# A skewed expert loop in a mixture-of-experts layer: gate/up of the next expert, then down of this one

## The reference, cut to what is computed

```python
def moe(xn, router_w, router_b, w_gate_up, b_gate_up, w_down, b_down):   # xn: 512 rows of 1024
    ...   # top 4 of 32 experts per row, softmax over the four, rows sorted by expert
    def expert_block(args):
        xb, e = args
        h = xb @ w_gate_up[e] + b_gate_up[e]            # 1024 -> 2048, gate and up interleaved
        gate = jnp.minimum(h[:, ::2], SWIGLU_LIMIT)
        up = jnp.clip(h[:, 1::2], -SWIGLU_LIMIT, SWIGLU_LIMIT)
        act = (up + 1.0) * (gate * jax.nn.sigmoid(SWIGLU_ALPHA * gate))
        return act @ w_down[e] + b_down[e]              # 1024 -> 1024
    ...   # each row's four outputs, weighted, are added to it

def reference(x, ...):
    h = x + hybrid_mixer(rmsnorm(x, ...), ...)
    h = h + moe(rmsnorm(h, ...), ...)
    return rmsnorm(h, norm_final_g)
```

## Time and profile before

| what | before |
|---|---|
| median of 3 runs | 2169.55 us (2169.14 to 2170.2) |
| span of the profiled execution | 2170.8 us |
| PE busy | 1977.2 us, 91% of the span, 9156 matmuls |
| PEld, DVE, ACT busy | 74%, 68%, 55% of the span |
| DMA | 489.15 MB, mean 225 GB/s |
| expert stage on PE | first bias matmul at 869.88 us, last matmul at 2136.58 us |

### The profile page before, as it was taken

The page is one execution under the profiler, slowest core; times in us unless marked ns, Lnnn a source line. Parts: engine busy times, 40 slices in busy tenths (PEclk is TensorE's granted clock), DMA queues, the critical chain, the costliest instruction groups (busy, mean ns, idle before and its releaser), DMA issues. The chain is left out here.

```text
span 2170.8 us, 27072 instructions
## 1 busy us (share of the span) xinstructions
PE 1977.2 (91%) x9156; PEld 1610.2 (74%) x9157; DVE 1482.3 (68%) x1727; ACT 1183.8 (55%) x1102; POOL 107.7 (5%) x90
## 2 busy tenths in 40 slices
PE   4997899999999984999999999999999999999993
PEld 3885588888788874777777777777777777777772
DVE  3324344324532433899899898998998998989984
ACT  3333222223443221776777777777777777677772
POOL 0000000000000000000000100000001000000001
PEclk7999899989999995999999999999999999999997
DMA  4221122201023319899999999999999999999962
GB/s 159 78 77 40 60 77 97 92 0 54 1 78 97 136 47 343 294 333 334 322 339 330 328 333 331 332 330 330 339 329 324 344 329 329 333 327 336 337 232 83
DMA packets 148314, 489.15 MB, mean 225 GB/s; under 512 B 15392, under 2 KB 17056, under 8 KB 148080
## 3 DMA queue, kind: packets, MB, share of 16 engines
q1 hardware_dynamic: 139056, 471.79, 62.5%
q0 software_dynamic: 9216, 16.81, 3.1%
HBM read 482.24 MB, written 23.07 MB: 233 GB/s over the span
## 5 line engine op out<-in xcount | busy, mean ns | idle before, releaser
L1371 DVE TENSOR_TENSOR expert_lo<-expert_chunk,expert_hi 128x2048 fp32r<-128x2048 f32 x384 | 874.9, 2289 | 107.9 <-ACT expert_hi L1366 107.9
L1366 ACT CAST expert_hi<-expert_chunk 128x2048 fp32r<-128x2048 f32 x384 | 730.1, 1905 | 244.0 <-PE psum L1488 240.8
L1488 PE MATMUL psum<-expert_hi,rowsT_hi 128*128 128x512 f32 x1024 | 323.3, 397 | 2.0 <-DVE expert_lo L1371 2.0
L1488 PE MATMUL psum<-expert_lo,rowsT_hi 128*128 128x512 f32 x1024 | 317.5, 391 | 0.0
L1488 PE MATMUL psum<-expert_hi,rowsT_lo 128*128 128x512 f32 x1024 | 316.0, 390 | 0.0
L327 DVE TENSOR_TENSOR chunk_lo<-chunk,chunk_hi 128x2048 fp32r<-128x2048 f32 x48 | 109.9, 2290 | 277.9 <-ACT chunk_hi L323 277.9
L1488 PEld LDWEIGHTS psum<-expert_lo,rowsT_hi 128*128 128x128 f32 x1024 | 192.8, 188 | 41.9
L1488 PEld LDWEIGHTS psum<-expert_hi,rowsT_lo 128*128 128x128 f32 x1024 | 192.7, 188 | 41.7
L1488 PEld LDWEIGHTS psum<-expert_hi,rowsT_hi 128*128 128x128 f32 x1024 | 188.0, 189 | 38.4 <-DVE expert_lo L1371 2.7
L353 PE MATMUL psum<-chunk_hi,xT_hi 128*128 128x512 f32 x480 | 188.9, 394 | 1.6 <-PEq L131 1.6
L353 PE MATMUL psum<-chunk_hi,xT_lo 128*128 128x512 f32 x480 | 188.1, 392 | 0.0
(11 more groups left out here) (226 smaller groups left out, 2365.7 us busy)
## 6 DMA issues: line engine op xcount, KB each, us to landing
expert_chunk<-in_expert_w_gate_up SPq DMA_DIRECT2D x256, 1024.0 KB, 7.3
expert_chunk<-in_expert_w_down SPq DMA_DIRECT2D x128, 1024.0 KB, 6.9
chunk<-in_w_in SPq DMA_DIRECT2D x38, 1024.0 KB, 5.1
chunk<-in_w_branch_gla SPq DMA_DIRECT2D x4, 1024.0 KB, 5.1
chunk<-in_w_mix_out SPq DMA_DIRECT2D x4, 1024.0 KB, 5.1
x_sb<-in_x SPq DMA_DIRECT2D x4, 512.0 KB, 6.0
chunk<-in_w_branch_att SPq DMA_DIRECT2D x2, 1024.0 KB, 5.1
h_sb<-in_x SPq DMA_DIRECT2D x1, 2048.0 KB, 9.9
```

Source lines behind the costliest of these rows:

```text
L1366: act.copy(whi[j % self.SLOTS][:], raw[j][:]).then_inc(S["hi"], 1)
L1371: dve.tensor_tensor(wlo[s][:], raw[j][:], whi[s][:].bitcast(F32), ALU.subtract).then_inc(S["lo"], 1)
L1488: last = pe.matmul(bank, x[:, row, :], w[s][:, kk, i * COLS:(i + 1) * COLS], start=False, stop=(k == self.PER_HALF - 1 and kk == 1 and x i ...
```

## The change

Each turn of the loop (a body) does the eight gate/up chunks of expert e + 1 and then the four down chunks of expert e. Gate/up of expert 0 stands ahead of the loop, down of expert 31 behind it; 31 bodies lie between, two written out, 27 as nine turns of three, two written out. Around this:

- A gate/up chunk is one k-tile of 128 rows by all 2048 columns, read in pieces of 8 KB. It needs four PSUM banks at once (0 to 3). A down chunk is as before. Bytes, chunks and matmuls per expert are the same.
- The ring has 9 buffers in place of 12, there are 4 slots in place of 3.
- PE waits for the high part, does eight matmuls, then waits for the low part and does four.
- `swiglu_in`, `swiglu_p`, `swiglu_out` and `gate_sigmoid` work on 1024 columns at once, four instructions on DVE for sixteen, one on ACT for four. PE turns all eight blocks of activations after chunk q = 2 of the next body (`turn_act`).
- Rows are listed and gathered two experts ahead in place of one; so there are three index, weight and pick tiles. `rows_out`, which writes an expert's output for the scatter, comes after chunk q = 3 of the next body on ACT.

```diff
-                self.first_expert = [self.sem(f"expert_chunk_loaded{j}") for j in range(self.CHUNKS)]
-                self.expert_ring = [self.sb(moe, f"expert_chunk{j}", [P, 2, self.WIDE]) for j in range(self.CHUNKS)]
+                self.chunk_loaded = [self.sem(f"expert_chunk_loaded{j}") for j in range(self.RING)]
+                self.expert_ring = [self.sb(moe, f"expert_chunk{j}", [P, 2, self.WIDE]) for j in range(self.RING)]
...
-                for j in range(2):
-                    sp.dma_start(self.expert_ring[j][:], self.expert_weights(0, j)).then_inc(self.first_expert[j], 16)
+                for k in range(2):
+                    self.load_gate_up(sp, k, 0, k)
                 sp.wait_ge(S["hn_done"], NB)
                 sp.dma_start(self.normed.rearrange("(b p) n -> p b n", p=P), hn[:]).then_inc(S["stored"], 16)
-                for j in range(2, self.EARLY):
-                    sp.dma_start(self.expert_ring[j][:], self.expert_weights(0, j)).then_inc(self.first_expert[j], 16)
+                for k in range(2, self.GU):
+                    self.load_gate_up(sp, k, 0, k)
+                self.load_gate_up(sp, self.GU, 1, 0)
                 sp.wait_ge(S["stored"], 32)
...
-    CHUNKS, PER_HALF, SLOTS, WIDE = 12, 4, 3, 1024
-    EARLY = 9
+    CHUNKS, PER_HALF, WIDE = 12, 4, 1024
+    RING, SLOTS = 9, 4
+    GU, PER_BODY, UNROLL = 8, 12, 3
...
+    def body_chunk(self, e, q):
+        return self.GU + self.PER_BODY * e + q
+
+    def load_gate_up(self, sp, c, e, k):
+        src = self.t["expert_w_gate_up"][0][bass.ds(e, 1), k * P:(k + 1) * P, :]
+        self.load_chunk(sp, c, src.rearrange("a p (k n) -> p (a k) n", k=2))
+
+    def load_down(self, sp, c, e, q):
+        src = self.t["expert_w_down"][0][bass.ds(e, 1), 2 * q * P:(2 * q + 2) * P, :]
+        self.load_chunk(sp, c, src.rearrange("a (k p) n -> p (a k) n", p=P))
+
+    def load_chunk(self, sp, c, src):
+        r = c % self.RING
+        sp.dma_start(self.expert_ring[r][:], src).then_inc(self.chunk_loaded[r], 16)
...
+        def hi(act, c, i=0):
+            act.wait_ge(loaded[c % RING], 16 * (TURN // RING) * i + 16 * (c // RING + 1))
+            act.wait_ge(S["slots_free"], TURN * i + c + 1)
+            act.copy(whi[c % SLOTS][:], raw[c % RING][:]).then_inc(S["hi"], 1)
+
+        def lo(dve, c, i=0):
+            s = c % SLOTS
+            dve.wait_ge(S["hi"], TURN * i + c + 1)
+            dve.tensor_tensor(wlo[s][:], raw[c % RING][:], whi[s][:].bitcast(F32), ALU.subtract).then_inc(S["lo"], 1)
...
+        def gate_up_chunk(pe, c, i, k, u):
+            s = c % SLOTS
+            if k == 0:
+                for m, bank in enumerate(h_banks):
+                    pe.matmul(bank, pick[u][:], bias[:, m * COLS:(m + 1) * COLS], start=True, stop=False)
+            pe.wait_ge(S["hi"], TURN * i + c + 1)
+            for x in (x_hi, x_lo):
+                for m, bank in enumerate(h_banks):
+                    pe.matmul(bank, x[:, k, :], whi[s][:, m // 2, m % 2 * COLS:(m % 2 + 1) * COLS], start=False, stop=False)
+            pe.wait_ge(S["lo"], TURN * i + c + 1)
+            for m, bank in enumerate(h_banks):
+                last = pe.matmul(bank, x_hi[:, k, :], wlo[s][:, m // 2, m % 2 * COLS:(m % 2 + 1) * COLS], start=False,
+                                 stop=(k == KT - 1))
...
+        def body_pe(pe, e0, i):
+            e, more = i * self.UNROLL + e0, e0 < E - 2
+            for q in range(BODY):
+                c = self.body_chunk(e0, q)
+                if q == 0:
+                    pe.wait_ge(S["x_lo"], 2 * e + 4)
+                    pe.wait_ge(S["picked"], e + 2)
+                    pe.wait_ge(S["gu"], 2 * e + 2)
+                if q < GU:
+                    gate_up_chunk(pe, c, i, q, (e0 + 1) % 3)
+                else:
+                    if q == GU:
+                        pe.wait_ge(S["aT_lo"], 2 * e + 2)
+                        if more:
+                            pe.wait_ge(S["index"], 2 * e + 6)
+                        if e0:
+                            pe.wait_ge(S["y_out"], 2 * e)
+                    down_chunk(pe, c, i, q - GU, e0 % 3)
+                if q == 2:
+                    turn_act(pe, e)
+                if q == 3 and more:
+                    list_rows(pe, e + 2, late=e0 > 0)
+                if q == 9 and more:
+                    turn_rows(pe, e + 2)
...
+        def rows_out(act, e0, i, u):
+            e = i * self.UNROLL + e0
+            for m in range(2):
+                act.wait_ge(S["slots_free"], TURN * i + self.body_chunk(e0, BODY - 1) + 1 + SLOTS)
+                if e0:
+                    act.wait_ge(S["scattered"], 16 * e)
+                act.activation(y[:, m * COLS:(m + 1) * COLS], y_banks[m], ACT.Copy,
+                               scale=weight[u][:, 0:1]).then_inc(S["y_out"], 1)
+
+        def body_act(act, e0, i):
+            e = i * self.UNROLL + e0
+            for q in range(BODY):
+                hi(act, self.body_chunk(e0, q), i)
+                if q == 0:
+                    turned_hi(act, e + 1, S["x_turned"], S["x_hi"], x_hi)
+                if q == 1:
+                    gate_sigmoid(act, e, first=e0 == 0)
+                if q == 3 and e0:
+                    rows_out(act, e0 - 1, i, (e0 - 1) % 3)
+                if q == 7:
+                    turned_hi(act, e, S["act_turned"], S["aT_hi"], a_hi)
+
+
+
+        def swiglu_in(dve, e, c, i, first=False):
+            dve.wait_ge(S["slots_free"], TURN * i + c + 1 + SLOTS)
+            if not first:
+                dve.wait_ge(S["act"], e)
+            halves = lambda v: v[:].rearrange("p (b n) -> p b n", b=4)
+            dve.tensor_scalar(halves(gv), gates_ups[:, :, :, 0], SWIGLU_LIMIT, None, ALU.min).then_inc(S["gu"], 1)
+            dve.tensor_scalar(halves(uv), gates_ups[:, :, :, 1], SWIGLU_LIMIT, -SWIGLU_LIMIT, ALU.min,
+                              ALU.max).then_inc(S["gu"], 1)
+
+        def swiglu_p(dve, e):
+            dve.wait_ge(S["gu"], 2 * e + 2)
+            dve.scalar_tensor_tensor(out=uv[:], in0=uv[:], scalar=1.0, in1=gv[:], op0=ALU.add,
+                                     op1=ALU.mult).then_inc(S["p"], 1)
...
+        def body_dve(dve, e0, i):
+            e, more = i * self.UNROLL + e0, e0 < E - 2
+            for q in range(BODY):
+                lo(dve, self.body_chunk(e0, q), i)
+                if q == 0:
+                    turned_lo(dve, e + 1, S["x_hi"], S["x_lo"], x_hi, x_lo)
+                    swiglu_p(dve, e)
+                if q == 1:
+                    swiglu_out(dve, e, first=e0 == 0)
+                if q == 2 and more:
+                    list_hot(dve, e + 2)
+                if q == 7:
+                    turned_lo(dve, e, S["aT_hi"], S["aT_lo"], a_hi, a_lo)
+                    if more:
+                        list_index(dve, e + 2, (e0 + 2) % 3, reused=e0 > 0)
+                        pick_bias(dve, e + 2, (e0 + 2) % 3)
+                if q == 10:
+                    swiglu_in(dve, e + 1, self.body_chunk(e0, GU - 1), i)
...
+        PEELED, LAST = 2, E - 1
+        TURNS = (LAST - PEELED) // self.UNROLL
+
+        def over_bodies(engine, body):
+            for e0 in range(PEELED):
+                body(engine, e0, 0)
+            with engine.Fori(0, TURNS) as i:
+                for u in range(self.UNROLL):
+                    body(engine, PEELED + u, i)
+            for e0 in range(PEELED + self.UNROLL * TURNS, LAST):
+                body(engine, e0, 0)
...
+                def body(sp, e0, i):
+                    e = i * self.UNROLL + e0
+                    for q in range(BODY):
+                        c = self.body_chunk(e0, q)
+                        if c < RING:
+                            continue
+                        sp.wait_ge(S["lo"], TURN * i + c - RING + 1)
+                        if q < GU:
+                            self.load_gate_up(sp, c, e + 1, q)
+                        else:
+                            self.load_down(sp, c, e, q - GU)
+                over_bodies(sp, body)
+                for q in range(4):
+                    c = self.body_chunk(LAST, q)
+                    sp.wait_ge(S["lo"], c - RING + 1)
+                    self.load_down(sp, c, LAST, q)
...
+                first = self.body_chunk(LAST, 0)
+                hi(act, first)
+                gate_sigmoid(act, LAST)
+                rows_out(act, LAST - 1, 0, (LAST - 1) % 3)
+                for c in range(first + 1, first + 4):
+                    hi(act, c)
+                turned_hi(act, LAST, S["act_turned"], S["aT_hi"], a_hi)
...
+                pe.wait_ge(S["x_lo"], 2)
+                pe.wait_ge(S["picked"], 1)
+                for c in range(GU):
+                    gate_up_chunk(pe, c, 0, c, 0)
+                turn_rows(pe, 1)
+                over_bodies(pe, body_pe)
+                first = self.body_chunk(LAST, 0)
+                turn_act(pe, LAST)
+                pe.wait_ge(S["aT_lo"], 2 * E)
```

(3 more changed lines are left out.)

324 lines of the change are left out of this document (121 added, 203 removed).

## The result

| what | before | after |
|---|---|---|
| median | 2169.88 us (2169.14 to 2170.46, 4 runs) | 2266.19 us (2259.73 to 2269.28, 4 runs) |
| ratio, 95% interval | | 1.0439 [1.0422, 1.0456] |
| span of the profiled execution | 2170.8 us | 2257.6 us |
| POOL busy | 107.7 us | 512.6 us |

The changed kernel is 4.4% slower. The forecast, 2103 us with a range of 2095 to 2148, was wrong, and on the wrong side.

The account below looks back on a forecast made before the run. PE's own work plus its waits for the swiglu was taken as the bound. Start, 31 bodies of 36.9 us (1144) and end summed to 2070.1 against 2137.0, a gain of 66.9 us: forecast 2103 us, range 2095 to 2148.

Parts of the forecast that it names:

- Do the waits go?: Loop body: checked whether PE's waits all vanish, so that a body takes 36.9 us in place of 39.54.
- indices are ready at 18.6: Gather in the body: issued about 1 us later, landed at 27.6, wanted at 30.4; room 2.8 us, the tightest wait.
- four slots leave 8.2: Splits in the body: four slots give 8.2 us for a chunk's split, where three gave 5.45.
- 34.8 against 36.9: DVE's work per body, 34.8 us, against PE's 36.9; it fits with 2.1 us of room.
- small steps: PE's work per body: 0.14 us added to 36.77 for steps not resolved, giving 36.9.
- the order over four banks: PE's matmuls: between nothing and 1.0 us per body, 31 us in all; taken as nothing.
- Start: Ahead of the loop: PE begins at about 870.6 us, not 869.88; 5.7 us before the first body, turning covers 0.8.
- End: Behind the loop, ahead of the last down: 10.5 us with PE idle for all but 0.8.
- Rival 1: Loop transfers: DMA becomes the bound, a body takes 38.35 us, 2148 us in all; chance 0.20.
- rival 4: Gate/up loads: 8 KB pieces cost more engine time, a body 43.9 us, 2320 us in all; chance 0.06.
- Rival 2: Turning of rows: gather landing grows to 12 us, PE waits 1.2 a body, 2140 us in all; chance 0.07.
- Rival 3: DVE in the loop doesn't keep up, a body takes 39.5 us, 2170 to 2185 us in all; chance 0.04.

Follow-up runs that it names:

- the single fill: The changed kernel with one fill of a 128x1 tile on DVE behind the split of q = 3; 2102.2 us, ratio 0.9682 to the kernel before.
- the halves: The changed kernel with the single fill, and each chunk's load cut into two of half the size; 2102.66 us, ratio 0.9689 to the kernel before.
- three slots: The changed kernel with three slots for split chunks in place of four, and the last expert's splits reordered; 2217.9 us, ratio 1.0222 to the kernel before.
- mended ends: The changed kernel with the single fill, and splits and copies reordered at the loop's start and end; 2092.61 us, ratio 0.9642 to the kernel before.
- six index tiles: The changed kernel with six index and weight tiles in place of three, loop unrolled six times; 2109.01 us, ratio 0.9717 to the kernel before.

## Why the prediction was wrong

**The step that failed** is "Do the waits go?". It goes through activations, rows, splits, DVE's sum, ACT, gather and loads, and leaves out the scatter. For the gather it says "indices are ready at 18.6": that took the index step to wait for nothing but the listing, while `list_index` also waits for the scatter of the expert before, to free its index tile. In the kernel before this wait was short (9.0 us in 16 places) and the earlier trace rows don't carry it. Worked out from rows of before, it should have been a term: the scatter starts with split 3 and lands 9.3 later, before the index step, so even priced at that it would have come out at nothing. What made it a loss is a second thing that no term covers: an issue's length was taken as its own property (1.73 us), while it depends on what DVE runs beside it.

**The same step had its cause in hand.** I took "four slots leave 8.2" as pure gain and the sum "34.8 against 36.9" as the only question about DVE. The 0.90 us ahead of the split at 1313.91 was for me idle time to be removed. It was the opening through which POOL's issue came. DVE's wait for ACT fell from 96.4 us to 8.9 in the same window, as I wanted, and the missing gaps cost 164 us (2266.2 against 2102.2 with the fill). The row of the changed kernel, 900 to 2050 us:

```profile
DVE expert_lo L1382 <- ACT expert_hi L1377: 8.9, 12, 1.3
```

**Without the starvation, the terms hold.** With the single fill the loop is the one forecast:
- Period: 36.78 us from bias matmul to bias matmul in 27 of the 30 bodies so measured (the others 37.15, 37.30, and 38.52 for the first), forecast 36.77 and 0.14 for "small steps". The 0.14 was not there, and the order over four banks costs nothing.
- DVE's sum: 188.07 of 200 us, 94%, as forecast; the 1024-column instructions start 1.13 us apart, estimated 1.17.
- Start: PE began at 869.90, and at 870.70 in the changed kernel (870.6), the first body after a wait of 4.98 (4.9).
- End: PE idle 10.20 us ahead of the last down product (10.5 less 0.8).
- Transfers: 0.96 share at 355 GB/s, forecast above 350.
- Total: 2102.2 measured for that kernel, 2103 forecast for the changed one. That it fits to 1 us is in part luck: the span is 2100.2, 3.7 under the forecast 2103.9, and the median stands 2.0 above it where the forecast took it to stand 1.25 below.

**The rivals.** Rival 1 (DMA the bound) and rival 4 (8 KB pieces dearer) are refuted by the single fill, where a body takes 36.78 at a share of 0.96 (rival 1 wanted 38.35), and by the halves, with which queue 1 took 61.6% of the engines' time for 60.5 and the time didn't change. Rival 2, the late gather, came as a consequence (31.5 us in 23 places), through indices that came late and not through slow packets (the rows landed 7.6 us after the start of their issue in the median, 8.0 before); by itself it showed with three slots. With the single fill they land after 9.8 us, 1.4 of it the longer issue of the gather: that takes 1.8 of the 2.8 us of room, a cost that the prediction did not have, and PE still waits for almost nothing. Rival 3 named DVE, but DVE was idle, not full. None named POOL's issue, and most of the 0.07 for "slower" rested on transfers. The signs that the prediction asked for settled it at once: the wait ahead of the down product, for `row_weight`, belongs to none of its cases.

The Trainium skill, "SBUF — State Buffer", section "Who interferes with whom", says that DVE and GpSimd share a pair of SBUF ports as an exclusive lock, and that a DVE instruction with two SBUF inputs contends with a GpSimd instruction that reads SBUF. Had I read the issue of the scatter, which reads its index tile, by that sentence, this would have been a rival. The runs agree with it where it says that such instructions keep GpSimd out. They differ where it takes `tensor_tensor` not to stall the generation of descriptors (it calls the reason inferred): here it stalled it for up to 15 us. They also leave open why a copy with one SBUF input didn't let POOL in.

## What to carry to other kernels

Idle time of an engine that isn't the bound can still be what another engine lives on: before you remove it, look at what other engines get done in it, and for POOL-issued indirect transfers beside unbroken runs of two-input instructions on DVE. When a wait on a far semaphore (here the reuse of an index tile) costs nothing today, write down its slack all the same, and what its length depends on. And if a transfer's issue is starved, the cure can be a single instruction: a 59 ns fill in the right place was worth 164 us here.

## What the runs showed of the hardware

- The issue of an indirect scatter with addition on POOL ended some 1.5 us behind an opening in DVE's run of instructions with two SBUF inputs. Enough were an idle stretch (0.06 to 0.07 us in 24 issues with six index tiles), a split with an input in PSUM, and a fill of 128x1 (0.06 us), which also made the next split 0.01 us late. Not enough were the bare ends of splits at full pace (592 of them, 2.201 to 2.205 us from start to start), and a copy of 128x128 with one SBUF input (0.22 us). At three bare ends where the next split came 0.01 to 0.05 us late, it got in.
- The issue of a gather was held as well, by less: 1.02 us where the split of the turned rows ran beside it (865.66 in the run with mended ends), 2.60 where weight splits did (864.73 with the single fill), 2.4 in the loop. It got in at the bare end of the first split.
- A count that POOL's sequencer raises behind an indirect transfer doesn't wait for its issue: it was passed while the issue had some 10 us to go.
- A pair of matmuls has the same pace over four banks in turn as over two: four matmuls in 0.91 us (1345.27 to 1346.18 with the single fill), where two pairs took 2 x 0.4544 before.
